# First block's attention: scaled probabilities and feature-major values, with the jobs, the fills and the convolution reordered

## What is computed

```python
u = rmsnorm(h, norm_mix_pre)
bg, cg, xin, q, kc, vc, ksl, vsl, kw, vw, gl = split(u @ w_in)
z = cg * xin                                  # convolution branch, 512 wide
y_conv = bg * causal_conv(z, conv_w)          # 3 taps along the tokens
# attention: 8 heads of 64, 2 groups of keys and values, 3 branches with gates of a token and a head
o_c = masked_softmax(q @ compress(kc).T) @ compress(vc)   # 31 compressed positions
o_s = masked_softmax(q @ selected keys.T) @ selected values
o_w = masked_softmax(q @ window keys.T) @ window values
y_att = g[0] * o_c + g[1] * o_s + g[2] * o_w
mixed = concat([rmsnorm(y_conv, norm_conv_out), rmsnorm(y_att, norm_attn_out)])
h = h + rmsnorm(mixed @ w_out, norm_mix_post)
```

## Time and profile before

| what | us |
|---|---|
| median of 3 runs | 2242.54 |
| lowest, highest | 2242.09, 2244.86 |
| the profiled execution | 2238.4 |
| its span in the profile | 2236.5 |

### The profile page before, as it was taken

How to read it: one execution, slowest core, us unless ns; L and a number is a source line. 1 busy time by engine, 2 the same in 40 slices (tenths; PEclk the granted TensorE clock), 3 DMA queues, 4 the chain that set the end, 5 groups by cost and what they waited for, 6 DMA issues and landing times.

```text
span 2236.5 us, 28991 instructions
## 1 busy us (share of the span) xinstructions
PE 2210.1 (99%) x11244; PEld 1805.3 (81%) x11244; DVE 1284.1 (57%) x1956; ACT 846.0 (38%) x1299; POOL 259.3 (12%) x281
## 2 busy tenths in 40 slices
PE   9999999999999999999999999999999999999999
PEld 7887788898888898886678888888887668888887
DVE  6468656445444226999874444332889874544422
ACT  5545454354333225223544333222322633433311
POOL 3000032120000001022231000011003232000000
PEclk9999999999999999999999999999999999999999
DMA  6221033123222222221122222223321122322222
GB/s 221 103 76 57 20 120 126 57 76 113 94 94 94 104 103 83 102 76 57 57 76 94 94 94 100 106 96 108 109 79 57 39 76 76 119 104 97 94 104 84
DMA packets 30484, 203.44 MB, mean 91 GB/s; under 512 B 3504, under 2 KB 4144, under 8 KB 6704
## 3 DMA queue, kind: packets, MB, share of 16 engines
q1 hardware_dynamic: 29088, 197.34, 24.7%
q10 hardware_dynamic: 1296, 4.72, 0.6%
HBM read 199.95 MB, written 2.10 MB: 90 GB/s over the span
## 4 chain that ended last, share of the span: by engine, by line
PE 87%; DVE 9%; issue 2%; ACT 1%; POOL 1%; DMA 0%; ACTq 0%; DVEq 0%; POOLq 0%
PE bank L418 25%; PE bank L420 25%; PE bank L419 25%; DVE cy L2361 3%; PE bank L2161 1%; PE bank L1005 1%; PE bank L2140 1%; DVE w_lo L304 1%; PE bank L2148 1%; PE bank L976 1%; POOL acc L327 1%; PE bank L2040 1%; PE bank L993 1%; DVE bank L2374 1%; PE bank L518 1%
## 5 line engine op out<-in xcount | busy, mean ns | idle before, releaser
L418 PE MATMUL bank<-x_hi,w_hi 128*128 128x512 f32 (+1 forms) x2032 | 789.9, 389 | 5.5 <-DVE x_lo L1777 2.3
L420 PE MATMUL bank<-x_hi,w_lo 128*128 128x512 f32 (+1 forms) x2032 | 775.0, 381 | 0.0
L419 PE MATMUL bank<-x_lo,w_hi 128*128 128x512 f32 (+1 forms) x2032 | 774.1, 381 | 0.0
L304 DVE TENSOR_TENSOR w_lo<-w_raw,w_hi 128x2048 fp32r<-128x2048 f32 x167 | 386.3, 2313 | 408.8 <-ACT w_hi L300 408.8
L300 ACT ACTIVATE w_hi<-w_raw 128x2048 fp32r<-128x2048 f32 x167 | 319.7, 1916 | 586.9 <-PE bank L420 585.0
L418 PEld LDWEIGHTS bank<-x_hi,w_hi 128*128 128x128 f32 x2032 | 382.1, 188 | 83.7 <-issue 6.6
L420 PEld LDWEIGHTS bank<-x_hi,w_lo 128*128 128x128 f32 x2032 | 381.9, 188 | 74.4
L419 PEld LDWEIGHTS bank<-x_lo,w_hi 128*128 128x128 f32 x2032 | 382.5, 188 | 72.7 <-issue 2.9
L418 PE MATMUL bank<-f_hi,w_hi 128*128 128x512 f32 (+1 forms) x572 | 213.3, 373 | 0.0
L419 PE MATMUL bank<-f_lo,w_hi 128*128 128x512 f32 (+1 forms) x572 | 213.2, 373 | 0.0
L420 PE MATMUL bank<-f_hi,w_lo 128*128 128x512 f32 (+1 forms) x572 | 213.2, 373 | 0.0
(11 more groups left out here) (360 smaller groups left out, 2624.0 us busy)
## 6 DMA issues: line engine op xcount, KB each, us to landing
w_raw<-w_d SPq DMA_DIRECT2D x184, 1024.0 KB, 4.8
out_d<-h SPq DMA_DIRECT2D x8, 256.0 KB, 6.5
h<-x_d ACTq DMA_DIRECT2D x3, 512.0 KB, 9.3
tab<-rope_d ACTq DMA_DIRECT2D x2, 768.0 KB, 4.2
memT<-mem_d ACTq DMA_DIRECT2D x1, 1024.0 KB, 4.8
w_raw<-w_d SPq DMA_DIRECT2D x2, 256.0 KB, 4.2
h<-x_d ACTq DMA_DIRECT2D x2, 256.0 KB, 5.9
w_raw<-w_d SPq DMA_DIRECT2D x1, 512.0 KB, 6.6
```

Source lines behind the costliest of these rows:

```text
L304: dve.tensor_tensor(w_lo[:, u.slot, :], w_raw[:, u.slot, :], w_hi[:, u.slot, :], ALU.subtract).then_inc(lo_ready, 1)
L418: pe.matmul(dst, wh[:, k, cols], hi[:, kx_, at:at + width], start=start, stop=False)
L419: pe.matmul(dst, wh[:, k, cols], lo[:, kx_, at:at + width], start=False, stop=False)
L420: return pe.matmul(dst, wl[:, k, cols], hi[:, kx_, at:at + width], start=False, stop=stop)
```

## The change

Six things are done.

1. Values go feature-major. One `values(q)` for each pair of heads and block takes both branches and the compressed one: 16 of them. For each head, a 64-column slice of the values is stationary and 128 turned probabilities move; all branches accumulate into bank 6, head e in partitions 64e to 64e+63. DVE copies the 128 x 128 result into `o_all`, which is feature-major now. `c_values`, `c_combine` and the multiply-adds of `combine` go.
2. Probabilities are scaled before they are turned: by ACT in two operations of each job (`scaled`), and by POOL in the compressed branch. DVE makes the weights of the step before ahead of the maxima of this one.
3. Turns and copies are three steps behind; `prob` and the turned probabilities have three buffers.
4. Jobs go with the pair of heads outside and the blocks inside, in the order 3, 0, 2, 1.
5. The gated projections go in the order cg, xin, bg; fills from 5 on all use bank 7, and a fill that waited for `fill_out` of its number less one waits for its own number. The fills end at step 17. The taps of the convolution go to steps 0 to 9, its gates to 10 to 17, its sum to 19, its rows to 24, and the memory's transfer to 18.
6. The norm of the attention output is made feature-major: squares of a feature tile (ACT), a sum over the tiles (DVE), column sums and a spread (PE), a multiplication by the row in bank 6 (DVE). `mixed_turn` goes. In step 32 and after, the products with `w_out` stand where the last turns and values are.

```diff
-        LAG_TURN, LAG_VALUES = 1, 2
+        LAG_J, PAIRS = 3, QB * 4
 
         U_VC = 4
         GATED = (5, 8, 11, 12, 13, 14)
-        GATED_BANK = (7, 6, 7, 6, 5, 7, 5, 7, 5, 7, 5, 7)
-        GATED_AT = {-4: 3, -3: 3, -2: 3, -1: 3, 0: 3, 1: 3, 2: 3, 3: 3, 4: 3, 5: 3, 6: 3, 7: 3,
-                    8: 2, 9: 2, 10: 2, 11: 2, 12: 2, 13: 2, 14: 2, 15: 2, 16: 2, 17: 2, 18: 2, 19: 2}
+        GATED_BANK = (7, 6, 7, 6, 5) + (7,) * 7
+        GATED_AT = {-4: 4, **{t: (3, 3, 2)[(t + 3) % 3] for t in range(-3, 18)}}
         GATED_BEFORE = 36
         assert GATED_BEFORE + sum(GATED_AT.values()) == 8 * len(GATED_BANK)
         GATED_END, _n = {}, GATED_BEFORE
...
             GATED_END[_t] = range(_n // 8, (_n + _c) // 8)
             _n += _c
 
-        SPLIT_AT = {0: (14, 0), 1: (14, 1), 6: (15, 0), 7: (15, 1), 14: (16, 0), 15: (16, 1), 22: (17, 0), 23: (17, 1)}
-
-        CONV_AT = {8: 0, 9: 2, 12: 4, 13: 6, 17: 8, 18: 10, 20: 12, 21: 14}
-        CONV_SQ_AT = {11: (0,), 16: (1,), 19: (2,), 22: (3,)}
-        AT_CONV_SUM, AT_CONV_INV, AT_CONV_ROWS = 23, 24, 27
-        CONV_NORM_AT = {27: (0, 1), 28: (2, 3)}
-        CONV_HI_AT = {28: (0, 1), 29: (2, 3)}
-        CONV_LO_AT = {29: (0, 1), 30: (2, 3)}
+        SPLIT_AT = {0: (14, 0), 1: (14, 1), 6: (15, 0), 7: (15, 1), 13: (16, 0), 14: (16, 1), 18: (17, 0), 19: (17, 1)}
+
+        CONV_TAPS_AT = {0: (0, 1), 3: (2, 3), 4: (4, 5), 5: (6, 7), 6: (8, 9), 9: (10, 11)}
+        CONV_GATE_AT = {10: 0, 12: 1, 16: 2, 17: 3}
+        CONV_SQ_AT = {11: (0,), 13: (1,), 17: (2,), 18: (3,)}
+        CONV_ADD_AT = {14: 1, 18: 2, 19: 3}
+        AT_CONV_SUM, AT_CONV_INV, AT_CONV_ROWS = 19, 20, 24
+        CONV_NORM_AT = {24: (0, 1), 25: (2, 3)}
+        CONV_HI_AT = {25: (0, 1), 26: (2, 3)}
+        CONV_LO_AT = {26: (0, 1), 27: (2, 3)}
...
+        BLOCK_ORDER = (3, 0, 2, 1)
+
         def job(j):
 
-            return j // 8, j % 8 // 2, j % 2, j % 8 // 4
+            m = j // 8
+            return BLOCK_ORDER[j // 2 % 4], m, j % 2, m // 2
+
+        def width(j):
+            return (job(j)[0] + 1) * P
 
         def wide(j):
-            return j >= 16
+            return job(j)[0] >= 2
 
         def turned_by_dve(j):
 
-            return max(0, j - 15)
+            return sum(wide(i) for i in range(j + 1))
+
+        def prob_of(j):
+            return prob[:, j % 3, :, :] if j % 3 < 2 else prob3[:, :, :]
+
+        def turned_of(j):
+            return probT[:, j % 3, :, :] if j % 3 < 2 else sq[:, :, :]
+
+        def value_pair(t):
+
+            if t == JOBS + 2:
+                return PAIRS - 1
+            return (t - 5) // 2 if t % 2 and 5 <= t < JOBS + 2 else None
...
-                            pe.wait_ge(fill_out, f - 1)
+                            pe.wait_ge(fill_out, f)
...
+            def values(q):
+
+                i, m, _, g = job(2 * q)
+                pe.wait_ge(j_pta, QB + 2 * q + 2)
+                if wide(2 * q):
+                    pe.wait_ge(j_ptd, turned_by_dve(2 * q + 1))
+                if q == 0:
+                    pe.wait_ge(vblk_ready, 4)
+                else:
+                    pe.wait_ge(j_o, q)
+                dst = [bank[HD * e:HD * e + HD, 6, 0:P] for e in range(2)]
                 for e in range(2):
-                    c0 = (j % 2) * 2 * HD + e * HD
+                    pe.matmul(dst[e], vblk[:, m * HD:(m + 1) * HD], pt_c[:, i, e * P:(e + 1) * P], start=True, stop=False)
+                for br in range(2):
                     for k in range(i + 1):
-                        mm = pe.matmul(bank[:, 6, c0:c0 + HD], probT[:, j % 2, e, k * P:(k + 1) * P],
-                                       vtok[:, k, br * P + g * HD:br * P + (g + 1) * HD], start=(k == 0), stop=(k == i))
+                        v = vtok[:, k, br * P + g * HD:br * P + (g + 1) * HD]
+                        for e in range(2):
+                            mm = pe.matmul(dst[e], v, turned_of(2 * q + br)[:, e, k * P:(k + 1) * P],
+                                           start=False, stop=(br == 1 and k == i))
...
+                if -QB <= t - LAG_J < 0:
+                    c_turn(t - LAG_J + QB)
+                elif t - LAG_J >= 0:
+                    turn(t - LAG_J)
                 gated_chunks(GATED_AT.get(t, 0))
                 if t == -QB:
                     compressed_values()
                 if t == JOBS:
                     pe.wait_ge(mix_lo, 4)
-                    pe.wait_ge(lo_ready, U_OUT + 1)
+                    pe.wait_ge(lo_ready, U_OUT + 2)
+                    pe.wait_ge(j_exp, QB + 2 * (JOBS - 1))
                 if t >= JOBS:
-                    mixed_products(0, (t - JOBS,), range(4))
-                if -QB <= t - LAG_TURN < 0:
-                    c_turn(t - LAG_TURN + QB)
-                elif 0 <= t - LAG_TURN < JOBS:
-                    turn(t - LAG_TURN)
-                if -QB <= t - LAG_VALUES < 0:
-                    c_values(t - LAG_VALUES + QB)
-                elif t - LAG_VALUES >= 0:
-                    values(t - LAG_VALUES)
+                    mixed_products((t - JOBS) // 2, ((t - JOBS) % 2,), range(4))
+                if value_pair(t) is not None:
+                    values(value_pair(t))
...
+            column_sums(pe, bank[:, 7, 0:QB], o_sq[:, :], ctmp[:, 1, :]).then_inc(ao_step, 1)
             mixed_products(2, (0,), range(4))
-            mixed_turn(0)
-            mixed_turn(1)
+            pe.wait_ge(ao_step, AO_INV)
+            pe.wait_ge(j_o, PAIRS)
+            spread(pe, bank[:, 6, :], small[:, 36:40]).then_inc(ao_step, 1)
...
+            def scaled(j):
+                act.wait_ge(j_w, j + 1)
+                act.wait_ge(j_scaled, QB + j)
+                for e in range(2):
+                    p = prob_of(j)[:, e, 0:width(j)]
+                    mul = act.activation(p, p, ACT.Copy, scale=jsm(j, 8, e))
+                mul.then_inc(j_scaled, 1)
...
-            for t in range(-QB, JOBS + LAG_TURN):
+            for t in range(-QB, JOBS + LAG_J):
+                if -QB <= t - LAG_J < 0:
+                    c_copy(t - LAG_J + QB)
+                elif t - LAG_J >= 0:
+                    copy_turned(t - LAG_J)
+                if 0 <= t - 1 < JOBS:
+                    scaled(t - 1)
                 if t < 0:
                     c_e(t + QB)
                 elif t < JOBS:
                     if t == 0:
                         act.wait_ge(unit_done, 11)
                     exps(t)
...
+            def weights(j):
                 i, m, br, g = job(j)
                 dve.wait_ge(j_exp, QB + 2 * (j + 1))
                 dve.reciprocal(jsm(j, 6), jsm(j, 4)).then_inc(j_rec, 1)
                 dve.wait_ge(j_rec, j + 1)
                 dve.tensor_tensor(jsm(j, 8), jsm(j, 6), gate[:, i, 6 * m + 1 + br:6 * m + 5 + br:3], ALU.mult).then_inc(j_w, 1)
-                dve.wait_ge(j_w, j + 1)
-                dve.wait_ge(j_pv, QB + j + 1)
-                for e in range(2):
-                    o = o_all[:, i, (2 * m + e) * HD:(2 * m + e + 1) * HD]
-                    if br:
-                        dve.wait_ge(j_o, QB + 2 * (j - 1) + e + 1)
-                    else:
-                        dve.wait_ge(j_o, i + 1)
-                    c0 = (j % 2) * 2 * HD + e * HD
-                    dve.scalar_tensor_tensor(out=o, in0=bank[:, 6, c0:c0 + HD], scalar=jsm(j, 8, e), in1=o,
-                                             op0=ALU.mult, op1=ALU.add).then_inc(j_o, 1)
+
+            def values_out(q):
+                i, m, _, g = job(2 * q)
+                dve.wait_ge(j_pv, q + 1)
+                dve.tensor_copy(o_all[:, m, i * P:(i + 1) * P], bank[:, 6, 0:P]).then_inc(j_o, 1)
+
+            def add_squares(m):
+                dve.wait_ge(ao_sq, m + 1)
+                dve.tensor_tensor(o_sq[:, :], ctmp[:, 0, :], ctmp[:, 1, :] if m == 1 else o_sq[:, :], ALU.add).then_inc(ao_sum, 1)
...
+            for t in range(-QB, JOBS + LAG_J + 1):
+                if -QB <= t - 1 < 0:
+                    c_weights(t - 1 + QB)
+                elif 0 <= t - 1 < JOBS:
+                    weights(t - 1)
                 if t < 0:
                     c_softmax(t + QB)
                 elif t < JOBS:
                     maxima(t)
-                if -QB <= t - LAG_TURN < 0:
-                    c_weights(t - LAG_TURN + QB)
-                elif 0 <= t - LAG_TURN < JOBS and wide(t - LAG_TURN):
-                    copy_turned(t - LAG_TURN)
-                if -QB <= t - LAG_VALUES < 0:
-                    c_combine(t - LAG_VALUES + QB)
-                elif t - LAG_VALUES >= 0:
-                    combine(t - LAG_VALUES)
                 for f in GATED_END.get(t, ()):
                     gated_out(f)
+                if 0 <= t - LAG_J < JOBS and wide(t - LAG_J):
+                    copy_turned(t - LAG_J)
+                if value_pair(t - 1) is not None:
+                    values_out(value_pair(t - 1))
+                if t in (22, 30):
+                    add_squares(t // 8 - 1)
...
```

(46 more changed lines are left out.)

172 lines of the change are left out of this document (64 added, 108 removed).

## The result

The changed kernel takes 2244.93 us (median of 20 runs, 2242.05 to 2250.75), the kernel before 2241.45 (20 runs). The ratio is 1.0019, with an interval of 1.0013 to 1.0024: slower by 4.2 us by the ratio, with the medians 3.5 apart, and just under the 0.2% named above. Forecast were 4.6 us less. The span of the profiled execution is 2243.3 us.

What follows compares the result with a forecast made beforehand. TensorE (PE), busy 99% of the span, was taken as the bound. Terms -15.4 + 0.8 - 4.1 + 1.6 + 4.1 + 8.4 = -4.6 us took 2242.5 to 2237.9; own range 2232 to 2243, outer range 2229 to 2246.

Steps and rivals of the forecast that it cites:

- rival C: Tail: waits from ACT to DVE cost nearer 0.5 us than 0.04, adding 5.5: 2243.4, no change; chance 0.17.
- Values, norm, old waits: PE's work: feature-major values -15.4 us, norm of the attention output +0.8, old hand-over waits replaced -4.1.
- Rival E: Value groups: the two heads don't run beside one another, +20.5 us, 8.3 hidden by tail gaps: 2250.1; chance 0.07.
- Fill 3: Second half of the second gated projection: PE waits until DVE has finished fill 2, +1.6 us.
- Compressed steps: PE waits for the third softmax (1.9), fill 5's output (1.65) and at step 3 (0.5): +4.1 us.
- Tail: Steps 18 to 31: softmax loop and other work need 41.7 us against PE's 33.3, +8.4 in gaps.
- the column sums: Tail, step 20: the convolution's sums stand in the softmax loop's way for 1.25 us.
- The clock: No term in the sum; a granted clock under 1.0 in the tail was listed as showing the forecast wrong.
- A: Rival, tail covered: PE's values and scores run beside the loop, the 8.4 us doesn't appear: 2229.5; chance 0.18.
- D: Rival: softmax loop with scaling bounds every step; tail gives 11.0 us, steps 3 to 17 6.8: 2255.7; chance 0.08.
- the gap that was put to the change of tiling mode: Ahead of each value group: 0.1 us gap, within 0.25 fixed per group, 4.0 in all, included in the sum.
- GpSimd's contention with VectorE: Compressed steps: shared SBUF interfaces slow DVE beside GpSimd's scaling; taken as covered, if not 0.9 us.

Runs made afterwards that it cites:

- e8: e5 with the value matmuls done head by head instead of alternating between heads; ratio 1.0016 to the kernel before.
- e3: Changed kernel with DVE's softmax of a compressed step ahead of the weights of the step before; ratio 0.9997 to the kernel before.
- e5: Changed kernel with the edits of e2, e3 and e4 together; 2231.6 us, ratio 0.9963 to the kernel before.
- e10: e5 with DVE's copies of value results and turned probabilities ahead of its weights and maxima; ratio 0.9963 to the kernel before.
- e12: e10 with six idle matmuls in two PE waits, ahead of the scores of steps 27 and 31; ratio 0.9958 to the kernel before.
- e7: e5 with the last three fills spread to step 20, convolution and last half splits moved along, root's rows at step 26; ratio 0.9978 to the kernel before.
- e11: e7 with the spread of the convolution's root at step 27 and the scalings behind it one step later; ratio 0.9958 to the kernel before.
- e4: Changed kernel with the convolution's column sums at step 21 for 19, and what follows them two steps later; ratio 0.9991 to the kernel before.
- e1: Changed kernel with idle matmuls filling four of PE's longest waits; ratio 0.9997 to the kernel before.
- e2: Changed kernel with fills 2 and 3 waiting for the output they waited for before the change; ratio 1.0007 to the kernel before.

## Why the prediction was wrong

The stretch was forecast at -4.6 and came out at +4.00, 8.6 apart. That 2244.93 lies in the outer range of 2229 to 2246, close to rival C's 2243.4, is chance: what C supposed didn't happen. By the steps of the sum:

- **Values, norm, old waits** (-15.4 + 0.8 - 4.1 = -18.7). Right in size: with the waits and the clock's 5.0 taken out, what remains of the stretch is -17.6. The group of block 2 was priced at 1.77 with its gap and took 1.68 and a gap of 0.1. Rival E fell, and e8 shows what it would have cost: 14.8 us of work (the 20.5 of its bound was a slip besides, as 96 x 0.21 is 20.2).
- **Fill 3** (+1.6): 1.58 in the trace, and 1.19 when it is undone. Right, and no fall of the clock stands behind it.
- **Compressed steps** (+4.1): 2.04 + 1.75 + 0.16 = 3.95 at two of the three forecast places, and but for 0.68 gone with the order (e3). Right in sum.
- **Tail** (+8.4): nine waits of 10.3 as noted, about 11.0 with 0.08 for each. Of the 2.6 too little, 2.2 are the column sums, the term that I had put at 1.25. These rows show how it came about: the last square begins only at 216.26, behind the scaling, the exponentials and a half split of its step on ACT (the gate that it needs ended at 211.56); and GpSimd's addition took 2.25 us and not 1.27, beside DVE's half split. It ended 1.1 us behind the end of that split (218.10 to 219.21), as it does in e5, e10 and e12; in e7 and e11, where no split stands beside it, it took 1.27.

```profile
215.31 1.05 ACT L813 ACTIVATE w_hi<-w_raw 128x1024 fp32r<-128x1024 f32 x1
216.26 0.63 ACT L1275 ACTIVATE z<-cv 128x512 f32<-128x512 f32 x1
...
216.88 1.22 DVE L821 TENSOR_TENSOR w_lo<-w_raw,w_hi 128x1024 fp32r<-128x1024 f32 x1
...
212.51 1.27 POOL L2629 TENSOR_TENSOR z<-z 128x512 f32<-128x512 f32 x1 [15.21 <-ACT z L1275]
216.96 2.25 POOL L2629 TENSOR_TENSOR z<-z 128x512 f32<-128x512 f32 x1 [3.19 <-ACT z L1275]
```

  The rest of the tail, 6.9 once the sums are moved (e4, e5), is about what the loop was forecast to leave (8.4 less the 1.25).
- **The clock**: the step that failed. The sum charged each wait its length and nothing more; a lower clock stood only in the list of what would prove it wrong. It cost 5.0 (e1). The waits that were forecast came, within 2.6 us; without the clock's 5.0 the stretch would have come out at -1.0, inside the forecast's own range. It isn't the total of the waits that decides: e5 keeps 6.9 us of them from step 18 on, with the clock at 1.00.

The difference is 5.0 of clock, 2.6 of tail and 1.1 of work, less 0.15 at the compressed steps: 8.6. No rival said so: A, C, D and E all kept the clock at 1.0. No wait stood in steps 5 to 17, so D fell. Hand-overs from ACT to DVE took 0.03 to 0.04 (207.58 to 207.62), so C fell. A tail without gaps (A) didn't come either.

It could have been read beforehand. I looked at the clock in the stretch of the change, where PE never rested for more than 0.7 us. In the second block of the same trace of before stands the pattern itself, a column sum that waits for GpSimd (timeline of PE, then the stretches around it):

```profile
1056.89 1.05 PE L336 MATMUL bank<-ones,la 128*128 128x1 f32 x8 [1.73 <-POOL la L2644]
```

```profile
1056.00:1058.00 2.00, 1.11 (x10) 1.09 (x12) 1.92 (x9) 0.69 (x3) 1.58 (x3) 1.00 0.00 0
1058.00:1060.00 2.00, 2.00 (x10) 1.02 (x12) 0.68 (x2) 1.74 (x4) 0.00 (x0) 0.50 0.01 4
1060.00:1062.00 2.00, 2.00 (x15) 1.17 (x12) 1.71 (x8) 0.66 (x1) 0.74 (x2) 0.64 0.02 4
```

A wait of 1.73 us, and the clock is at half for over 3 us after it. Priced by this row, a forecast wait of this size would have been dearer by some 1.5 to 2 us, an estimate; three such, as came to pass, by 5 or 6, and the forecast would have been no change. Which three of the forecast waits it would be, the row couldn't say: behind that at fill 3 the clock stayed at 1.00.

Of the two rules of the Trainium skill that the prediction names (TensorEngine Tiling (Array Packing), Key Properties, and GPSIMD Engine Reference, Specifications), the gap that was put to the change of tiling mode is there (0.1 ahead of a group) and was in the sum. GpSimd's contention with VectorE was weighed at the wrong place. At the compressed steps DVE's small operation took 0.35 for 0.17, and once, at 135.83, this stands right ahead of the subtraction that PE waited 2.04 for, so that 0.18 of that wait are its. At the column sums GpSimd lost 1.0 us, in a wait of PE. The rule as the prediction puts it, for operations with two inputs, bears on the split there; the slower small operations, the 0.52 of the earlier trace rows among them, have one input.

## What to carry to other kernels

A wait of PE can have two prices: its length, and what runs behind it at half the clock. Before a wait of a microsecond or two is accepted in a stretch where PE never rested, look in the whole trace for a wait of that size and read the granted clock behind it; 6.9 us of idle time in eleven pieces (e5) were cheaper than 5.4 in eight, two of them of 1.6 (e10). When a change that makes the work smaller comes out slower, list the new waits by size and undo them one by one: here three edits, to one wait, one order and one position (e5), turned 4.2 us lost into 8.3 gained, with the change itself left as it is.

## What was not expected

- Idle matmuls in waits bring 5.0 us (e1) and 2.0 us (e12).
- The fall is not tied to one wait's length: 1.99 us at step 32 are followed by half clock in the changed kernel and not in e4 and e5, while 1.56 us are in e10; and 1.36 with 1.04 are in e2 and not in the changed kernel. What decides it these runs don't show.
- The cost of a fall varies: about 7 us at low clock around the column sums in e3, 3.4 us in the changed kernel, for the same wait of 3.36.
- GpSimd's addition of 128x512 takes 1.27 us, and 2.25 when it begins just behind the start of a two-input operation of DVE of 1.22.
